# Quads two bodies earlier, an index decode by masks in PSUM, and other places for VectorE's low halves in a trunk's PEER layers

## The chip, the cores and the metric

The kernel runs on one core of a Trainium2 chip. The metric is the device time of one execution in microseconds (us). Each count given as "x" is a number of instructions. Five engines work beside each other and wait for each other by semaphores: TensorE (PE), VectorE (DVE), ScalarE (ACT), GpSimd (POOL) and SyncE (SP), which issues the DMA transfers.

## The reference

A decoder trunk of two layers on x of 256 tokens by 1024 channels, all float32. A layer adds two things to x. The first is a mixer (retention, RWKV-7 and gated linear attention behind one projection). The second is PEER, a retrieval over 128 x 128 = 16,384 experts of one neuron each:

```python
q = (xb @ w_q).reshape(p, 8, 2, 128)
sc = jnp.einsum('thpc,hpnc->thpn', q, sub_keys)
s1, i1 = lax.top_k(sc[:, :, 0], 16)
s2, i2 = lax.top_k(sc[:, :, 1], 16)
cand = s1[..., :, None] + s2[..., None, :]
cand_idx = i1[..., :, None] * 128 + i2[..., None, :]
top_s, sel = lax.top_k(cand.reshape(p, 8, 256), 16)
gate = softmax(top_s)
act = gelu(einsum('td,ted->te', xb, u[eidx])) * gate
out = einsum('te,ted->td', act, v[eidx])
```

So each token has 8 heads with 16 chosen experts each. A token's expert is found by a row index i1 and a column index i2.

## The kernel before

**The dense form.** The kernel doesn't gather. It computes the activations of all 16,384 experts for all 256 tokens (u half), multiplies them with a dense matrix of gates that is zero where a token didn't choose an expert, and multiplies the result with all of v (v half). In each layer the u half comes in 32 **bodies** of four expert groups of 128, each body in eight **halves** m = 0 to 7 (four of the eight channel chunks each). Float32 weights are split in two parts of lower precision: ACT casts a half's weights from the ring w_ring into expert_hi (u_split, L976), DVE or POOL subtracts to make expert_lo (the **low**, L1656 on DVE, L1826 on POOL), and PE makes 12 products of 128x128 by 256 columns (u_half, L783 to L785). There are four buffers for the parts, so the cast of a half waits until PE has done the half four before it. The v half has the same form (v_split L1047, v_lows L1660, a_split L1056, a_lows L1664, v_half L814 to L816). SP reloads the two ring slots of 1 MB when the lows of their last halves are made.

**Who makes the lows.** In bodies 1 to FREE - 1 = 10, DVE makes the lows of halves 2 and 6 (D_FEW) by few_lows, at places written by hand into the sort, and POOL makes the other six (P_MANY). From body FREE = 11 on DVE makes six (D_MANY) and POOL two (P_FEW).

**The sort (topk, L1567).** While PE works on bodies 0 to 10, DVE takes the scores SC (32 rows of 128 per token tile set), and for two halves t of them finds the 16 largest of each row: 16 max operations, 16 pairs of max_index and match_replace, 16 max again, 16 max_index again. Then stage1_done is signalled, the 50 candidates per head are built (CAND, L1595 to L1605), and the 16 best with their places POS are found in the same way. The gates' differences are signalled (gdiff_ready). ACT takes the exponential at a fixed place of its own order, behind body EXP_BODY - 1 = 8 (L1217); DVE normalises in gates() (L1647), and PE turns the indices and gates (turn_sel) within body FREE.

**The decode.** POS counts through rows of unequal length (16, 8, 5, 4, ... candidates). To find row and column, DVE compares POS with all 16 row starts at once (ISROW, 2048 elements per tile), multiplies with row lengths, index steps and column indices, and reduces each product (L1634 to L1645), for two tiles of 8 heads.

**The quads.** From body QB = 12 on a body also holds three **quads**, each of which makes the gates of four tokens: DVE compares with an iota to get one-hot matrices (hots, L1670), ACT scales them by the gates in eight operations (gate_rows, L1009), PE multiplies (quad, L793 and L794, 8 products), and DVE multiplies the result into the activations (gated, L1678). There are 64 quads and 20 x 3 = 60 of them fit in the bodies; four stand behind the last body. Activations of the bodies before QB (LATE = 48 rows) go straight into ACTS; in later bodies gelu goes back to PSUM (L987) and u_muls (L1685) multiplies it with what the quads so far left in ACTS. For that, unwritten rows of ACTS hold ones: ACT writes them three rows in each body (ones, L1001), eight rows three times later, and POOL writes the rest (L1908). a_split of the first two v groups waits for the last quad and the last u_muls.

**The inverse (invert, L539).** Earlier in the layer the RWKV part inverts 12 triangular matrices of 128 by doubling blocks, level by level. For each level and each of two chunks k, PE makes Y = MASKED x TI (L550), DVE masks it (L1458), PE makes six pairs of small products with TT and Y (L562, L563), and DVE adds them to the halves of TI and TT (L1471). Behind the last level stand transposes (turn_out, L678) and the chunks, which read TT.

The constants of the plan are these:

```python
N_BODY, EXP_BODY, FREE, QB = 32, 9, 11, 12
N_QUAD = S // 4
N_LOOPED = 3 * (N_BODY - QB)
LATE = 4 * QB
```

## Time and profile before

| | us |
|---|---|
| median of 3 runs | 2248.65 |
| lowest and highest run | 2247.8, 2250.03 |
| the profiled execution, its own time | 2248.29 |
| its span, first to last instruction | 2246.5 |
| PE busy | 2128.1 (95%) |
| DVE busy | 1473.0 (66%) |
| ACT busy | 1312.9 (58%) |
| POOL busy | 438.2 (20%) |

The span is that of the profiled execution, from its first to its last instruction; the time is what the device took for the same execution. An engine is busy when one of its instructions runs; a busy time is a union, so overlapping instructions count once. TensorE's granted clock (PEclk) is a share of 2.4 GHz. "Idle before" in a group or a timeline row is how long the engine stood idle before those instructions, with the operation that ended the wait behind the arrow. In layer 0 the u half runs from 337.6 to 755.1 us and the v half from 765.6 to about 1117; layer 1 has the same at 1453.8 and 1883.9. Body 0 starts at 337.6 us, body 1 at 349.1, body 5 at 395.2, body 10 at 469.5 in layer 0.

### The profile page before, as it was taken

What the parts mean: (1) busy time and instruction counts of PE and PEld (TensorE: products, weight loads), DVE (VectorE), ACT (ScalarE), POOL (GpSimd) and SP (SyncE); (2) the same over time, 40 slices, a digit from 0 to 9 for tenths busy, and PEclk for the clock granted to TensorE, in tenths of its full rate; (3) what the DMA queues carried; (4) which work ended last, traced back from release to release, by engine and by line L of the source; (5) the groups of instructions that cost most, each with busy time, mean ns of one, the idle gap of its engine ahead of it and who ended that gap; (6) DMA issues with size and microseconds to landing.
All of it is one profiled execution on the core that took longest, in us unless ns stands there. A gap on an engine that the chain in (4) does not pass through costs nothing.

```text
span 2246.5 us, 45241 instructions
## 1 busy us (share of the span) xinstructions
PE 2128.1 (95%) x14596; PEld 1927.4 (86%) x14596; DVE 1473.0 (66%) x2926; ACT 1312.9 (58%) x3097; POOL 438.2 (20%) x358
## 2 busy tenths in 40 slices
PE   7899899899999899999898998997999998999997
PEld 7889599899999788888787885997999997888886
DVE  5764247968878666666567533489687886666665
ACT  5530145479999755555564302553899996555554
POOL 0312007752222100000004020176522220000000
PEclk9999799999999999999999997998999999999999
DMA  5310244344444355555542102453444443555555
GB/s 222 113 57 1 94 150 171 144 153 168 157 161 168 131 187 194 198 187 192 182 183 94 57 1 94 169 176 124 169 165 155 166 158 141 189 195 194 188 196 186
DMA packets 47459, 338.77 MB, mean 151 GB/s; under 512 B 5648, under 2 KB 5776, under 8 KB 6928
## 3 DMA queue, kind: packets, MB, share of 16 engines
q1 hardware_dynamic: 47376, 337.73, 41.5%
q8 instruction: 44, 0.72, 0.1%
q14 instruction: 39, 0.32, 0.0%
HBM read 336.66 MB, written 1.05 MB: 150 GB/s over the span
## 4 chain that ended last, share of the span: by engine, by line
PE 81%; DVE 8%; issue 4%; POOL 3%; ACT 2%; DMA 2%; DVEq 0%; SPq 0%; POOLq 0%; PEldq 0%; ACTq 0%
PE ps L814 10%; PE ps L815 10%; PE ps L816 10%; PE ps L783 9%; PE ps L785 8%; PE ps L784 8%; POOL expert_lo L1826 3%; PE ps L686 3%; PE ps L407 2%; PE ps L409 2%; PE ps L408 2%; PE ps L550 2%; PE ps L563 1%; PE ps L562 1%; PE ps L793 1%
## 5 line engine op out<-in xcount | busy, mean ns | idle before, releaser
L783 PE MATMUL ps<-h_t_hi,expert_hi 128*128 128x256 f32 x2048 | 595.7, 291 | 27.3 <-DVE expert_lo L1656 22.1
L784 PE MATMUL ps<-h_t_lo,expert_hi 128*128 128x256 f32 x2048 | 582.8, 285 | 0.0
L785 PE MATMUL ps<-h_t_hi,expert_lo 128*128 128x256 f32 x2048 | 582.4, 284 | 0.0
L1826 POOL TENSOR_TENSOR expert_lo<-w_ring,expert_hi 128x512 fp32r<-128x512 f32 x220 | 338.1, 1544 | 763.9 <-ACT expert_hi L976 760.4
L783 PEld LDWEIGHTS ps<-h_t_hi,expert_hi 128*128 128x128 f32 x2048 | 396.0, 193 | 31.9 <-issue 13.3
L814 PE MATMUL ps<-expert_hi,act_hi 128*128 128x512 f32 x1024 | 400.5, 391 | 4.8 <-DVE act_lo L1664 4.8
L815 PE MATMUL ps<-expert_lo,act_hi 128*128 128x512 f32 x1024 | 400.1, 391 | 0.0
L816 PE MATMUL ps<-expert_hi,act_lo 128*128 128x512 f32 x1024 | 400.0, 391 | 0.0
L784 PEld LDWEIGHTS ps<-h_t_lo,expert_hi 128*128 128x128 f32 x2048 | 396.3, 194 | 0.0
L785 PEld LDWEIGHTS ps<-h_t_hi,expert_lo 128*128 128x128 f32 x2048 | 395.9, 193 | 0.0
L976 ACT CAST expert_hi<-w_ring 128x512 fp32r<-128x512 f32 x512 | 308.9, 615 | 141.9 <-PE ps L785 129.1
L1660 DVE TENSOR_TENSOR expert_lo<-w_ring,expert_hi 128x512 fp32r<-128x512 f32 x512 | 331.1, 688 | 0.4
L1056 ACT CAST act_hi<-big 128x256 fp32r (+1 forms) x256 | 103.8, 406 | 329.2 <-PE ps L816 329.2
L1047 ACT CAST expert_hi<-w_ring 128x512 fp32r<-128x512 f32 x512 | 291.3, 617 | 0.0
L1656 DVE TENSOR_TENSOR expert_lo<-w_ring,expert_hi 128x512 fp32r<-128x512 f32 x292 | 213.2, 742 | 116.8 <-ACT expert_hi L976 113.4
L1664 DVE TENSOR_TENSOR act_lo<-big,act_hi 128x256 fp32r<-128x256 f32 x256 | 108.6, 425 | 261.6 <-ACT act_hi L1056 261.6
L814 PEld LDWEIGHTS ps<-expert_hi,act_hi 128*128 128x128 f32 x1024 | 193.3, 189 | 45.5 <-DVE expert_lo L1660 5.3
L815 PEld LDWEIGHTS ps<-expert_lo,act_hi 128*128 128x128 f32 x1024 | 193.3, 189 | 40.1
L816 PEld LDWEIGHTS ps<-expert_hi,act_lo 128*128 128x128 f32 x1024 | 193.1, 189 | 40.1
L938 ACT CAST expert_hi<-w_ring 128x512 fp32r<-128x512 f32 x168 | 99.8, 621 | 119.4 <-PE ps L425 54.5
L1316 DVE TENSOR_TENSOR expert_lo<-w_ring,expert_hi 128x512 fp32r<-128x512 f32 x168 | 119.3, 749 | 67.1 <-ACT expert_hi L938 64.8
L407 PE MATMUL ps<-h_t_hi,expert_hi 128*128 128x256 f32 x448 | 128.3, 286 | 2.4 <-DVE expert_lo L1316 1.0
(293 smaller groups left out, 3359.5 us busy)
## 6 DMA issues: line engine op xcount, KB each, us to landing
w_ring<-u_t SPq DMA_DIRECT2D x128, 1024.0 KB, 4.8
w_ring<-v_t SPq DMA_DIRECT2D x128, 1024.0 KB, 4.8
w_ring<-w_in SPq DMA_DIRECT2D x32, 1024.0 KB, 4.9
w_ring<-w_q SPq DMA_DIRECT2D x16, 1024.0 KB, 4.9
w_ring<-w_out SPq DMA_DIRECT2D x8, 1024.0 KB, 4.8
big<-xconst SPq DMA_DIRECT2D x2, 1666.0 KB, 9.3
w_ring<-keys SPq DMA_DIRECT2D x2, 1024.0 KB, 4.8
big<-rows SPq DMA_DIRECT2D x2, 576.0 KB, 11.3
```

The lines of the kernel that those rows point to most:

```text
L407: pe.matmul(o, w_hi_m[:, c, :], HTH[:, d, :], start=d == 0, stop=False)
L783: pe.matmul(o, w_hi[:, c, :], HTH[:, d, :], start=d == 0, stop=False)
L784: pe.matmul(o, w_hi[:, c, :], HTL[:, d, :], start=False, stop=False)
L785: mm = pe.matmul(o, w_lo[:, c, :], HTH[:, d, :], start=False, stop=d == DC - 1)
L814: pe.matmul(o, a_hi_t, EH[:, m % 4, :], start=start, stop=False, skip_group_check=True)
L815: pe.matmul(o, a_hi_t, EL[:, m % 4, :], start=False, stop=False, skip_group_check=True)
L816: mm = pe.matmul(o, a_lo_t, EH[:, m % 4, :], start=False, stop=True, skip_group_check=True)
L976: act.copy(EH[:, m % 4, :], RING[:, m // 4, (m % 4) * 512:(m % 4 + 1) * 512]).then_inc(u_hi, 1)
L1047: act.copy(EH[:, m % 4, :], RING[:, m // 4, (m % 4) * 512:(m % 4 + 1) * 512]).then_inc(v_hi, 1)
L1656: dve.tensor_tensor(EL[:, m % 4, :], RING[:, m // 4, (m % 4) * 512:(m % 4 + 1) * 512], EH[:, m % 4, :].bitcast(F32), ALU.subtract).then_in ...
L1660: dve.tensor_tensor(EL[:, m % 4, :], RING[:, m // 4, (m % 4) * 512:(m % 4 + 1) * 512], EH[:, m % 4, :].bitcast(F32), ALU.subtract).then_in ...
L1826: pool.tensor_tensor(EL[:, m % 4, :], RING[:, m // 4, (m % 4) * 512:(m % 4 + 1) * 512], EH[:, m % 4, :].bitcast(F32), ALU.subtract).then_i ...
```

## The change

The plan starts the quads at body 10 and ends them within body 31, so the constants move, and bodies 30 and 31 get forms of their own:

```diff
-N_BODY, EXP_BODY, FREE, QB = 32, 9, 11, 12
+N_BODY, EXP_BODY, FREE, QB = 32, 7, 9, 10
 N_QUAD = S // 4
-N_LOOPED = 3 * (N_BODY - QB)
+ONES = 5
@@ PE
-                with pe.Fori(QB, N_BODY) as j:
-                    u_and_quads(j)
-                for q in range(N_LOOPED, N_QUAD):
-                    quad(q % 3, q)
+                with pe.Fori(QB, N_BODY - 1) as j:
+                    u_and_quads(j, (1, 4, 6))
+                u_and_quads(N_BODY - 1, (1,))
@@ ACT
-                with act.Fori(QB, N_BODY - 1) as j:
-                    u_and_gates(j, False)
-                u_and_gates(N_BODY - 1, True)
-                for q in range(N_LOOPED + 2, N_QUAD):
-                    gate_rows(q % 3, q, 0, 8)
+                with act.Fori(QB, N_BODY - 2) as j:
+                    u_and_gates(j, 3, False)
+                u_and_gates(N_BODY - 2, 2, False)
+                u_and_gates(N_BODY - 1, 0, True)
@@ DVE
-                with dve.Fori(QB, N_BODY - 1) as j:
-                    u_and_gated(j, False)
-                u_and_gated(N_BODY - 1, True)
-                for q in range(N_LOOPED, N_QUAD):
-                    gated(q % 3, q, 128 - LATE)
-                    if q + 3 < N_QUAD:
-                        hots(q % 3, q + 3, False)
+                with dve.Fori(QB, N_BODY - 2) as j:
+                    u_and_gated(j, 3, 3, False)
+                u_and_gated(N_BODY - 2, 3, 1, False)
+                u_and_gated(N_BODY - 1, 1, 0, True)
```

ACT writes ones five rows a body instead of three. In the sort DVE's lows stand at other places: one for t = 0 (behind the second maxima) instead of three, four for t = 1 (in the middle of the first maxima, in the middle of the index and replace operations, behind them, and four operations into the second max_index) instead of five, then one behind the candidates, one in the middle of their index and replace operations, one behind their second maxima, one behind their second indices, and four in the decode instead of six. DVE makes 16 of them in all instead of 20.

The decode goes by overwriting. DECODE is a view of PSUM banks 0 to 3 as eight matrices of 256. One mask says where POS has reached row i, and one predicated copy then overwrites the picked value with that of row i:

```diff
+        DECODE = PS[:, 0:4, :].rearrange("p b n -> p (b n)").rearrange("p (m u n) -> p m u n", m=8, u=16)
@@ topk
+                def overwrite(dst, i, src):
+
+                    counted(dve.copy_predicated(dst[:, :, :], DECODE[:, i % 7, :, :].bitcast(U32), src.broadcast_to([P, 16, 16])))
+
+                for i in range(1, 17):
+                    if i < 16:
+                        counted(dve.tensor_scalar(DECODE[:, i % 7, :, :], at, float(ROW_AT[i]), None, ALU.is_ge))
+                    if i > 1:
+                        all_but(1 if i < 16 else 0)
+                        overwrite(PICK, i - 1, ROWKEY[:, :, i - 1:i])
+                    if i == 9:
+                        few_lows(1)
+                all_but(0)
+                few_lows(1)
...
+                for i in range(1, 17):
+                    if i < 16:
+                        counted(dve.tensor_scalar(DECODE[:, i % 7, :, :], at, 128.0 * (i - 1), None, ALU.is_gt))
+                    if i > 1:
+                        all_but(1 if i < 16 else 0)
+                        overwrite(I2F, i - 1, x[:, :, 1, i - 1:i])
+                    if i in (6, 14):
+                        few_lows(1)
+                all_but(0)
```

Here counted() raises the semaphore dve_step by one, and all_but(n) waits until all counted operations but the last n are done. Between the two loops stand five small operations of 256 elements that split the key (row start x 128 + i1) again. The ten products and comparisons of 2048 elements and the six reductions of before, on ISROW and PICKED, are gone.

At the inverse's last level (b = 64) the products and additions into TI are left out, since nothing reads TI after it:

```diff
-                            pe.matmul(PS[:, 4 + 2 * k, h * 64:(h + 1) * 64], TT[:, u, :], first, start=True, stop=True)
+                            if b < 64:
+                                pe.matmul(PS[:, 4 + 2 * k, h * 64:(h + 1) * 64], TT[:, u, :], first, start=True, stop=True)
@@ DVE
-                            ins = dve.tensor_tensor(half, half, zz, ALU.add)
+                            elif i == 1:
+                                half = dst[:, u0:u0 + NH, 64:128]
+                                ins = dve.tensor_tensor(half, half, z.rearrange("p (m b) -> p m b", b=64), ALU.add)
```

## Rows read from the trace of the kernel before

**Rows 1.** The page: the span, and busy time by engine.

```profile
span 2246.5 us, 45241 instructions
...
PE 2128.1 (95%) x14596; PEld 1927.4 (86%) x14596; DVE 1473.0 (66%) x2926; ACT 1312.9 (58%) x3097; POOL 438.2 (20%) x358
```

**Rows 2.** Windows: length; busy us (count) of PE, PEld, DVE, ACT, POOL; PEclk; DMA.

```profile
349.10:395.20 46.10, 46.10 (x386) 46.10 (x385) 38.74 (x212) 26.24 (x51) 31.30 (x24) 1.00 0.53 187
395.20:469.50 74.30, 63.50 (x482) 61.75 (x481) 70.05 (x163) 36.56 (x68) 54.64 (x30) 0.93 0.39 140
507.80:742.10 234.30, 234.30 (x2162) 231.98 (x2161) 190.84 (x291) 227.49 (x651) 55.68 (x36) 1.00 0.45 163
755.14:765.64 10.50, 2.90 (x34) 2.15 (x33) 6.69 (x12) 9.48 (x29) 0.00 (x0) 0.76 0.00 0
765.60:779.10 13.50, 13.46 (x49) 10.93 (x50) 6.58 (x12) 4.35 (x9) 0.00 (x0) 0.81 0.34 116
1511.40:1587.80 76.40, 64.02 (x483) 62.53 (x482) 72.03 (x163) 36.44 (x68) 54.61 (x30) 0.91 0.37 136
```

**Rows 3.** Groups: PE in 391.6 to 472, POOL in 349.1 to 395.2, then 395.2 to 469.5.

```profile
L783 PE MATMUL ps<-h_t_hi,expert_hi 128*128 128x256 f32 x177 | 52.8, 298 | 10.8 <-DVE expert_lo L1656 8.7 <-POOL expert_lo L1826 1.7 <-ACT big L981 0.4
...
L1826 POOL TENSOR_TENSOR expert_lo<-w_ring,expert_hi 128x512 fp32r<-128x512 f32 x24 | 31.3, 1306 | 14.6 <-ACT expert_hi L976 13.4
...
L1826 POOL TENSOR_TENSOR expert_lo<-w_ring,expert_hi 128x512 fp32r<-128x512 f32 x30 | 54.6, 1837 | 18.4 <-ACT expert_hi L976 17.6
```

**Rows 4.** Groups: DVE's lows in 337 to 389.6.

```profile
L1656 DVE TENSOR_TENSOR expert_lo<-w_ring,expert_hi 128x512 fp32r<-128x512 f32 x8 | 5.5, 692 | 12.8 <-ACT expert_hi L976 12.8
```

**Rows 5.** Timeline of DVE: start, us, operation [idle before <-what ended it].

```profile
348.56 0.69 DVE L1656 TENSOR_TENSOR expert_lo<-w_ring,expert_hi 128x512 fp32r<-128x512 f32 x1 [5.55 <-ACT expert_hi L976]
...
395.33 0.69 DVE L1656 TENSOR_TENSOR expert_lo<-w_ring,expert_hi 128x512 fp32r<-128x512 f32 x1
...
403.73 1.41 DVE L1656 TENSOR_TENSOR expert_lo<-w_ring,expert_hi 128x512 fp32r<-128x512 f32 x1
405.06 1.87 DVE L1616 MAX8 h_t<-big 128x8 f32<-128x50 f32 x16
...
411.47 1.16 DVE L1625 CAST h_t<-h_t 128x256 f32<-128x256 uint32 x1
412.66 3.27 DVE L1634 TENSOR_TENSOR big<-h_t,row_consts 128x2048 f32<-128x2048 f32 x1
...
419.27 1.63 DVE L1656 TENSOR_TENSOR expert_lo<-w_ring,expert_hi 128x512 fp32r<-128x512 f32 x1
...
460.80 2.29 DVE L1645 TENSOR_REDUCE h_t<-big 128x128 f32<-128x2048 f32 x1
```

**Rows 6.** Groups by form, DVE, whole span.

```profile
L1553 DVE COPY_PREDICATED big<-big,ps 128x512 f32<-128x512 uint32 x28 | 18.9, 729 | 21.0 <-PE ps L657 20.6 <-DVE big L1530 0.5
...
L1481 DVE COPY big<-ps 128x384 f32<-128x384 f32 x4 | 2.2, 558 | 11.0 <-PE ps L588 11.0
...
L1555 DVE COPY big<-ps 128x256 f32<-128x256 f32 x4 | 1.5, 417 | 0.0
...
L1328 DVE COPY big<-big 128x256 f32<-128x256 f32 x2 | 0.6, 294 | 0.1
```

**Rows 7.** Timeline of the end of the first half of PEER, layer 0.

```profile
755.34 0.37 ACT L987 ACTIVATE ps<-ps 128x256 f32<-128x256 f32 x1 [1.25 <-PE ps L785]
...
762.04 2.17 ACT L1047 CAST expert_hi<-w_ring 128x512 fp32r<-128x512 f32 x4
...
764.10 0.71 ACT L1056 CAST act_hi<-big 128x256 fp32r<-128x256 f32 x2
...
765.64 0.76 PE L814 MATMUL ps<-expert_hi,act_hi 128*128 128x512 f32 x1 [2.41 <-DVE act_lo L1664]
```

**Rows 8.** Timeline of PE: the inverse's last level and the transposes behind it.

```profile
203.34 0.33 PE L562 MATMUL ps<-big 128*128 128x64 f32 x2
...
208.65 1.26 PE L678 MATMUL ps<-const_sb,big 128*128 128x128 f32 x10
```

More of the change, by code:

```diff
@@ L215, in trunk @@
         CAND2 = big(16 * NC).rearrange("p (u n) -> p u n", u=16)
-        ISROW, PICKED = (big(2048).rearrange("p (u k n) -> p u k n", u=8, k=16) for _ in range(2))
-        STEP1 = IDX[:, 0:16, :]
+        ROWKEY = big(256).rearrange("p (u n) -> p u n", u=16)
         ht_flat = HT[:, :, :].rearrange("p c n -> p (c n)")
-        TOPV, POS, POSF, GATE, I1F, I2F, ROWAT, COLF = (ht_flat[:, 256 * i:256 * (i + 1)].rearrange("p (u n) -> p u n", u=16) for i in range(8))
+        TOPV, POS, PICK, GATE, I1F, I2F, PICKI, COLN = (ht_flat[:, 256 * i:256 * (i + 1)].rearrange("p (u n) -> p u n", u=16) for i in range(8))
         ACTS = BIG[:, :].rearrange("p (e t) -> p e t", t=S)
@@ L795, in quad, with u_and_quads @@
                 mm.then_inc(quad_done, 1)
-            def u_and_quads(j):
-                q = 3 * (j - QB)
+            def u_and_quads(j, after):
                 for m in range(8):
                     u_half(m, j, False)
-                    if m in (1, 4, 6):
-                        i = (1, 4, 6).index(m)
-                        quad(i, q + i)
+                    if m in after:
+                        i = after.index(m)
+                        quad(i, 3 * (j - QB) + i)
             def v_half(m, j, first):
@@ L1011, in gate_rows, with u_and_gates @@
                     ins.then_inc(hot_gate, 1)
-            def u_and_gates(j, last):
+            def u_and_gates(j, quads, last):
                 q = 3 * (j - QB)
@@ L1023, in u_and_gates @@
                 u_gelu_late(0, j)
-                gate_rows(2, q + 2, 0, 6)
+                if quads:
+                    gate_rows(2, q + 2, 0, 6)
                 split(6)
@@ L1027, in u_and_gates @@
                 split(7)
-                gate_rows(2, q + 2, 6, 8)
-                gate_rows(0, q + 3, 0, 4)
+                if quads:
+                    gate_rows(2, q + 2, 6, 8)
+                    gate_rows(0, q + 3, 0, 4)
                 split(8)
@@ L1032, in u_and_gates @@
                 u_gelu_late(2, j)
-                gate_rows(0, q + 3, 4, 8)
-                gate_rows(1, q + 4, 0, 2)
+                if quads:
+                    gate_rows(0, q + 3, 4, 8)
+                if quads == 3:
+                    gate_rows(1, q + 4, 0, 2)
                 split(10)
@@ L1037, in u_and_gates @@
                 split(11)
-                gate_rows(1, q + 4, 2, 8)
+                if quads == 3:
+                    gate_rows(1, q + 4, 2, 8)
             def v_split(m, j, first):
@@ L1214, in _ @@
                     u_body(j)
-                    ones(bass.ds(LATE - 3 + 3 * j, 3), 3)
+                    ones(bass.ds(LATE - ONES + ONES * j, ONES), ONES)
                 act.wait_ge(gdiff_ready, 1)
@@ L1580, in topk @@
                         ins = dve.match_replace(SC2[:, u % 16, :], VAL[:, u, 0:8], SC[:, u, :], NEG)
-                        if u % 16 == (7 if t else 11):
+                        if t and u % 16 == 7:
                             few_lows(1)
@@ L1685, in u_muls, with u_and_gated, quad_step, hot_step @@
                 dve.tensor_tensor(a, a, PS[:, 6 + e % 2, 0:S], ALU.mult).then_inc(u_mul, 1)
-            def u_and_gated(j, last):
+            def u_and_gated(j, quads, next_quads, last):
                 q, done = 3 * (j - QB), 4 * (j - QB)
+                def quad_step(i):
+                    if i < quads:
+                        gated(i, q + i, done + i)
+                def hot_step(i):
+                    if i < next_quads:
+                        hots(i, q + 3 + i, False)
+                def next_lows(m):
+                    if not last:
+                        u_lows(m, j + 1)
                 u_lows(4, j)
                 u_lows(5, j)
-                gated(0, q, done)
-                hots(0, q + 3, False)
+                quad_step(0)
+                hot_step(0)
                 u_lows(6, j)
-                u_muls(0, j, q + 1)
-                gated(1, q + 1, done + 1)
-                if not last:
-                    u_lows(0, j + 1)
-                hots(1, q + 4, False)
-                u_muls(1, j, q + 2)
-                if not last:
-                    u_lows(1, j + 1)
-                gated(2, q + 2, done + 2)
-                if not last:
-                    u_lows(2, j + 1)
-                hots(2, q + 5, False)
-                u_muls(2, j, q + 3)
-                u_muls(3, j, q + 3)
+                u_muls(0, j, q + min(1, quads))
+                quad_step(1)
+                next_lows(0)
+                hot_step(1)
+                u_muls(1, j, q + min(2, quads))
+                next_lows(1)
+                quad_step(2)
+                next_lows(2)
+                hot_step(2)
+                u_muls(2, j, q + quads)
+                u_muls(3, j, q + quads)
             norm_rows(0, HN)
```

59 lines of the change are left out of this document (29 added, 30 removed).

## The prediction

> **What bounds the kernel now.** I read the page first. TensorE (PE) is busy for 95% of the span [rows 1]; the reader is to see that only idle or slowed PE time can be won. The windows come second [rows 2]. A body without quads costs PE 46.10/4 = 11.52 us (1.44 us for each of its eight halves), a body with three quads 13.02 us (234.30 us for 18 of them), so a quad costs 1.50/3 = 0.50 us. Two stretches fall short. Bodies 5 to 9 take 74.30 us where five times 11.52 is 57.6: 16.7 us lost in layer 0, and in layer 1 76.40 - 57.6 = 18.8 us. Between the last product of the first half of PEER and the first of the second half lie 10.50 us, with the last four quads in them (the same in layer 1; one of the two rows stands). Third, the group rows for bodies 5 to 9 [rows 3]: PE's waits were ended mostly by DVE's low halves (L1656), and POOL's lows took 1.84 us each, against 1.31 us in bodies 1 to 4. While it sorts and decodes, DVE makes halves 2 and 6 of each body, and it is behind. The kernel is DVE-bound there and PE-bound nearly everywhere else.
>
> My sum goes against the profiled execution: 2248.3 us, of which 2246.5 is the span [rows 1]; it lies 0.4 us under the median of the runs shown, 2248.65.
>
> **Part 1, the inverse.** At the last level (b = 64) PE drops 12 of its 24 small products and DVE two of four additions. The 24 pairs run back to back from 203.34 to 208.65, when the next transposes start [rows 8]: 5.31 us. Half of that is **2.6 us per layer**, if DVE's masked rows, which feed the second half of the products, are ready as early as that; I estimate that they are, since PE doesn't wait there now. The ends are 1.3 us (one of two phases only) and 2.7 us.
>
> **Part 2, the end of the quads.** Bodies 10 and 11 get three quads each, body 31 keeps one, and the four behind the loop go: the same 64 quads, so PE's work is equal, but 4 x 0.50 = 2.0 us of it move out of the gap. What is left in the gap is a chain on ACT and DVE [rows 7]: the last gelu starts 0.2 us after PE's last product, whose end is the window's start (755.34 - 755.14), and ACT goes on 0.3 later (its 0.37 less an overlap); four casts of v take 764.10 - 762.04 = 2.06; the cast of the activations and its low half lead 1.54 us later to the first product (765.64 - 764.10), of which about 0.5 is DVE working off its last gated block, so 1.05. Sum 0.2 + 0.3 + 2.06 + 1.05 = 3.6 us. Gain 10.5 - 3.6 - 2.0 = **4.9 us per layer**. PE's granted clock fell from 2.4 towards 1.2 GHz in that gap (0.76 in the mean over it, 0.81 over the first v body's 13.5 us [rows 2]: 0.19 x 13.5 = 2.6 us of full clock lost there). A gap of 3.6 us may let it fall too; I count no change, with ends of 2 us won and 1 us lost per layer. ACT and DVE carry in bodies 10 and 11 what they carry in 12 to 29 now, and PE was full there: nothing. What the first body with quads costs over the others moves from body 12 to body 10: nothing.
>
> **Part 3, the lows in the sort.** DVE waited 12.8 us for casts before its low halves [rows 4], 5.55 of them before the first, at 348.56 [rows 5]. A low for half m of body j is wanted by PE at 349.1 + 11.52(j-1) + 1.44m, and its cast is there some 3.5 us earlier; one comes due every 5.76 us. With the first low behind the second maxima, DVE gets there at 348.2, and later waits come to about 0.3 us. Up to the low behind the candidates, now at 395.33, fall away 12.8 us of waits and three lows at 0.61; 0.4 + 0.3 of waits and 0.3 for a wider table are added: 395.33 - 12.8 - 1.8 + 1.0 = 381.7. But that low is now the sixth (body 3, half 6), wanted at 380.8.
>
> **Part 4, the decode.** It runs from 411.47 to 463.1 now, 51.6 us with six lows; the big operations of 2048 elements take 2.3 to 3.3 us [rows 5]. In its place come 15 masks and 15 overwrites, twice, of 256 elements. A copy of 256 from PSUM takes 0.417 [rows 6]. An overwrite of 512 takes 0.729; the step from 256 to 384 costs 0.141, so 256 fewer give 0.45. Neighbours overlap by 0.08 (a low ends at 405.14, the next operation starts at 405.06 [rows 5]), so a pair is 0.42 + 0.45 - 0.16 = 0.71, with the waits 0.72. Ends: 0.55, with a mask at the SBUF copy's 0.294 and an overwrite of 0.42; 0.95, if each wait drains DVE (no overlap, 0.04 for each). Sum: 30 x 0.72 = 21.6, steps between 3.0, four lows of 1.2 (between the 0.69 of a free one and the 1.41 and 1.63 of late ones [rows 5]) = 4.8: 29.4 instead of 51.6.
>
> First what the rows show of port and place: a copy of 256 takes 0.294 from SBUF and 0.417 from PSUM [rows 6]. The trace agrees with the Trainium skill (VectorE: DVE Perf Modes, "Why PSUM operands drop a tier"), which speaks against this change: a PSUM operand costs fp32 copies their double rate. By it masks in SBUF would be 0.12 us cheaper each, 3.7 us per layer. Against that stand POOL's lows, 1.31 us beside the sort and 1.84 beside the decode [rows 3]. The Trainium skill (SBUF — State Buffer, "🔬 SBUF: two separate sides") gives a lock that GpSimd shares with DVE operations of two SBUF inputs or a two-port mode; by it masks and overwrites with a PSUM side neither wait for POOL nor hold it up.
>
> **The stalls that stay.** Between the lows DVE has 1.9 us for 16 maxima, 5.9 for 16 index and replace operations (395.33 to 403.73 less a low and the maxima), 3.0 for the second indices (406.93 to 411.47 less a low and the difference of 0.5) [rows 5]. A late low costs 1.2, and every stall moves what PE wants next. Low by low (DVE's start, its end, PE's want, the stall):
> sixth 381.7, 382.8, 380.8: 2.0; seventh (1.9 + 2.9 on) 387.6, 388.8, 388.5: 0.3; eighth (2.9 + 1.9 on) 393.6, 394.8, 394.6: 0.2; ninth 397.8, in time, then 0.7 + 0.5 + 0.9 to the decode's start at 399.9; tenth (0.35 and 8 pairs) 406.0, 407.2, 406.3: 0.9; eleventh (7 pairs) 412.3, 413.5, 413.0: 0.5; twelfth (2.1, 0.35 and 5 pairs) 419.5, 420.7, 419.2: 1.5; thirteenth (8 pairs) 426.5, 427.7, 426.5: 1.2. Two more pairs and 1.5 for the gates end at 430.7, the fourteenth is wanted at 433.4, and the decode is over before body 9. **6.6 us per layer stay** of 16.7 and 18.8. Bounds: 2.5 (lows at 0.69, pair 0.60) and 12.6 (pair 0.95: 30 x 0.23 = 6.9 later, of which some 6 reach PE). Gain 10.1 + 12.2 = **22.3 us**. ACT now waits for the differences of the gates behind body 6, whose end is at 349.1 + 6 x 11.52 = 418.2 at the earliest; DVE has them at about 399: nothing, and should it come after 418, casts and so PE stop. ACT's five slices of ones instead of three per body fall into its idle time (26.2 of 46.1 us busy [rows 2]): nothing.
>
> **Sum.** 2248.3 - 5.2 - 9.8 - 22.3 = **2211.0 us**.
>
> **Rivals.**
> A, the forecast above: 0.66.
> B, nearly no stall stays (2.5 us per layer) and the clock holds in the gap: 2211.0 - 8.2 - 4 = 2199. For it: the 12.8 us of DVE's waits are simply gone [rows 4]; against: the sixth low is late by the order alone. 0.15.
> C, the decode is dearer: masks and overwrites drain each other at 1.1 us a pair, 30 x 0.38 = 11.4 us later per layer, stalls of about 18 as now. Only parts 1 and 2 are left: 2233. For it: every overwrite waits on a counter; against: a chained operation starts 0.03 us behind the one it waits for (412.63, 412.66 [rows 5]). 0.11.
> D, the gap doesn't shrink, since something else (v's transfer, the order of ACT's casts) holds the first product: 2221. 0.04.
> E, slower: overwrites stand behind POOL's lows. A DVE low grew from 0.69 to 1.63 beside busy POOL, by 0.94 us [rows 5]. If all 30 pairs paid it, the decode ends 28 us later and 6.6 + 28 = 34.8 us are lost per layer: 2248.3 - 15.0 + 69.6 - 35.5 = 2267. It decides from 1.34 us a pair (0.62 over mine), where the extra 18.6 us per layer use up all gains. Against: POOL is busy for only 54.64 of 74.30 us there [rows 2], and not every operation can meet it. 0.04.
>
> **Numbers.** About 0.2% (4.5 us) is what a measurement can tell from no change. The range takes in A with its bounds (2199 to 2225) and B; C and E are left out, with D inside. Faster 0.95, same 0.01, slower 0.04.
>
> **What would show it.** Bodies 5 to 8 (with body 3) should lose 6 to 7 us over 11.52 each, with PE's waits there still ended by the DVE low of halves 6; the gap between the halves of PEER should be 3.6 us with no quad in it; the overwrites should start 0.7 us apart; POOL's lows should be back at 1.3 us; the transposes behind the inverse should start at about 206.0. Wrong would be a pair over 1 us, a decode that ends behind 441 (the start of body 9), or a gap over 6 us.

## The result and the profile after

The changed kernel takes **2197.5 us** in the median of four runs (2193.7 to 2201.7), against 2248.7 before: ratio 0.977 (0.975 to 0.980), 51 us less where 37.3 were forecast. The time lies just under the range. One execution of inv_dve, further down, took 2951.1 us at a mean granted clock of 0.658 and is left out of its ratio. The profiled execution took 2193.71 us, 54.6 less than the one that the prediction summed against. The page of after:

```profile
PE 2094.9 (96%) x14548; PEld 1900.6 (87%) x14548; DVE 1442.1 (66%) x3050; ACT 1314.0 (60%) x3093; POOL 388.7 (18%) x342
PE 86%; DVE 9%; ACT 2%; DMA 2%; issue 1%; SPq 0%; DVEq 0%; ACTq 0%; PEldq 0%
L784 PE MATMUL ps<-h_t_hi,expert_hi 128*128 128x256 f32 x2048 | 591.3, 289 | 12.4 <-DVE expert_lo L1685 8.6
L1865 POOL TENSOR_TENSOR expert_lo<-w_ring,expert_hi 128x512 fp32r<-128x512 f32 x204 | 289.7, 1428 | 772.6 <-ACT expert_hi L975 770.9
```

To see where the 54.6 us went, I cut both executions at the first product of each half of PEER (u: first half, v: second):

| stretch | before | after | less | forecast |
|---|---|---|---|---|
| start to first u product, layer 0 | 337.6 | 328.8 | 8.8 | 2.6 |
| first u to first v product, layer 0 | 428.0 | 411.9 | 16.1 | 15.0 |
| last v body to first u product, layer 1 | 348.3 | 337.8 | 10.5 | 2.6 |
| first u to first v product, layer 1 | 430.1 | 411.8 | 18.3 | 17.1 |
| first v body, layer 0 (in layer 1 0.2 more, not less) | 13.4 | 12.6 | 0.8 | 0 |

The two stretches with parts 2 to 4 came out nearly as forecast: 34.4 us against 32.1. Of the 17.3 us beyond the forecast, 14.1 lie ahead of PEER (19.3 us against 5.2), where the change touches only the inverse. Windows of after: first bodies 5 to 9 with their transposes, in each layer (74.30 and 76.40 us before [rows 2]):

```profile
387.30:450.50 63.20, 59.39 (x488) 58.47 (x487) 40.94 (x89) 43.49 (x76) 36.24 (x25) 1.00 0.50 175
1476.10:1539.20 63.10, 59.37 (x489) 58.43 (x487) 40.85 (x89) 43.56 (x76) 36.31 (x25) 1.00 0.48 174
```

and the POOL group over the same stretch, whose mean was 1837 ns before [rows 3]:

```profile
L1865 POOL TENSOR_TENSOR expert_lo<-w_ring,expert_hi 128x512 fp32r<-128x512 f32 x24 | 31.7, 1329 | 27.5 <-ACT expert_hi L975 27.1
```

The gap between the halves, in the timeline of after (compare [rows 7]): no quad is left in it, and it lasts 3.5 us.

```profile
737.04 0.28 PE L786 MATMUL ps<-h_t_hi,expert_lo 128*128 128x256 f32 x1
737.36 0.37 ACT L986 ACTIVATE ps<-ps 128x256 f32<-128x256 f32 x1 [2.51 <-PE ps L786]
737.63 2.17 ACT L1051 CAST expert_hi<-w_ring 128x512 fp32r<-128x512 f32 x4
739.70 0.71 ACT L1060 CAST act_hi<-big 128x256 fp32r<-128x256 f32 x2
740.71 0.47 PE L814 MATMUL ps<-expert_hi,act_hi 128*128 128x512 f32 x1 [3.39 <-DVE act_lo L1693]
```

The decode on DVE (L1651 and L1668 make masks, L1647 overwrites): a pair every 0.68 us, start to start, from 390.07 to 417.9. The first row is the sixth low, ahead of it.

```profile
370.98 1.67 DVE L1685 TENSOR_TENSOR expert_lo<-w_ring,expert_hi 128x512 fp32r<-128x512 f32 x1
...
390.07 0.77 DVE L1651 TENSOR_SCALAR ps<-ps 128x256 f32<-128x256 f32 x2
390.74 0.45 DVE L1647 COPY_PREDICATED h_t<-ps,big 128x256 f32<-128x256 uint32 x1
391.08 0.44 DVE L1651 TENSOR_SCALAR ps<-ps 128x256 f32<-128x256 f32 x1
391.42 0.45 DVE L1647 COPY_PREDICATED h_t<-ps,big 128x256 f32<-128x256 uint32 x1
...
395.83 1.44 DVE L1685 TENSOR_TENSOR expert_lo<-w_ring,expert_hi 128x512 fp32r<-128x512 f32 x1
...
417.00 0.94 DVE L1647 COPY_PREDICATED h_t<-ps,big 128x256 f32<-128x256 uint32 x2
```

Not every stall that is left is DVE's. Bodies 3, 5 and 6 wait for its low halves; body 7 waits for ACT, whose exponential (L1221) stands behind body 6 now and has a table load of 1.28 us before and behind it. The waits of PE that end in these bodies, with ACT's two loads:

```profile
372.78 0.38 PE L784 MATMUL ps<-h_t_hi,expert_hi 128*128 128x256 f32 x1 [0.56 <-DVE expert_lo L1685]
397.40 0.38 PE L784 MATMUL ps<-h_t_hi,expert_hi 128*128 128x256 f32 x1 [1.25 <-DVE expert_lo L1685]
410.89 0.38 PE L784 MATMUL ps<-h_t_hi,expert_hi 128*128 128x256 f32 x1 [1.70 <-DVE expert_lo L1685]
416.14 1.28 ACT L1221 ACT_TABLE_LOAD   x1
418.90 1.28 ACT L980 ACT_TABLE_LOAD   x1
420.63 0.38 PE L784 MATMUL ps<-h_t_hi,expert_hi 128*128 128x256 f32 x1 [0.69 <-ACT big L980]
```

Now the inverse and the chunk part behind it. PE's timeline in after: the last level's small products take 2.63 us (205.11 to 207.74) instead of 5.31 [rows 8].

```profile
205.11 2.79 PE L564 MATMUL ps<-big 128*128 128x64 f32 x24
207.74 1.26 PE L679 MATMUL ps<-const_sb,big 128*128 128x128 f32 x10
209.96 1.55 PE L581 MATMUL ps<-big 128*128 128x64 f32 x12 [0.96 <-ACT h_t L1188]
```

The windows of the chunk part, from these transposes (L679) to the output projection's twelve matmuls that follow it. Columns: stretch, length, busy us of PE, PEld, DVE, ACT, POOL, PEclk, DMA. First before, then after:

```profile
208.65:241.35 32.70, 31.74 (x168) 24.87 (x167) 4.26 (x11) 1.41 (x4) 0.00 (x0) 0.74 0.00 1
```

```profile
207.74:233.08 25.34, 24.38 (x169) 19.14 (x168) 3.79 (x10) 1.41 (x4) 0.00 (x0) 0.99 0.00 1
```

The same products take 7.4 us less, since PE's granted clock was at 1.2 GHz for 20.5 us over this part before (224.6 to 245.1), and for 3.4 us at its end after (from 232.8). Such a stretch at 1.2 GHz is called a spell below, and those that begin over the chunk part are the long ones (17 to 24 us) or the short ones (3 to 7 us).

### The profile page after: what moved, and what is told of

It is laid out like the page before. It is cut to its first block, busy times and chain, and to the rows that moved or that the text cites. A ratio compares the mean times of both kernels' runs of the same rounds, so it can differ in the third digit from the quotient of the medians.

```text
span 2191.9 us, 45295 instructions
## 1 busy us (share of the span) xinstructions
PE 2094.9 (96%) x14548; PEld 1900.6 (87%) x14548; DVE 1442.1 (66%) x3050; ACT 1314.0 (60%) x3093; POOL 388.7 (18%) x342
## 4 chain that ended last, share of the span: by engine, by line
PE 86%; DVE 9%; ACT 2%; DMA 2%; issue 1%; SPq 0%; DVEq 0%; ACTq 0%; PEldq 0%
PE ps L814 11%; PE ps L815 11%; PE ps L816 11%; PE ps L784 10%; PE ps L786 9%; PE ps L785 9%; PE ps L687 2%; PE ps L407 2%; PE ps L408 2%; PE ps L409 2%; PE ps L550 2%; PE ps L564 1%; PE ps L794 1%; PE ps L423 1%; PE ps L795 1%; DVE expert_lo L1319 1%
## 5 line engine op out<-in xcount | busy, mean ns | idle before, releaser
L1865 POOL TENSOR_TENSOR expert_lo<-w_ring,expert_hi 128x512 fp32r<-128x512 f32 x204 | 289.7, 1428 | 772.6 <-ACT expert_hi L975 770.9
L784 PEld LDWEIGHTS ps<-h_t_hi,expert_hi 128*128 128x128 f32 x2048 | 391.6, 191 | 15.7 <-ACT big L980 8.4
L786 PEld LDWEIGHTS ps<-h_t_hi,expert_lo 128*128 128x128 f32 x2048 | 391.6, 191 | 0.0
```

The source lines that it names most:

```text
L784: pe.matmul(o, w_hi[:, c, :], HTH[:, d, :], start=d == 0, stop=False)
L786: mm = pe.matmul(o, w_lo[:, c, :], HTH[:, d, :], start=False, stop=d == DC - 1)
L1865: pool.tensor_tensor(EL[:, m % 4, :], RING[:, m // 4, (m % 4) * 512:(m % 4 + 1) * 512], EH[:, m % 4, :].bitcast(F32), ALU.subtract).then_i ...
```

## The experiments

**Splitting the change.** Edits: inv_only is the kernel before with only the inverse's edit; no_inv the kernel after with that edit taken back; inv_dve the kernel before with only DVE's two additions dropped.

```diff
 # inv_only, PE's part; no_inv is the reverse, on the kernel after
-                            pe.matmul(PS[:, 4 + 2 * k, h * 64:(h + 1) * 64], TT[:, u, :], first, start=True, stop=True)
+                            if b < 64:
+                                pe.matmul(PS[:, 4 + 2 * k, h * 64:(h + 1) * 64], TT[:, u, :], first, start=True, stop=True)
...
```

> The kernel before, with the inverse's part of the change alone. Theory C (clock): leaving out 12 products per layer saves 2 x 2.65 us of PE time and also shortens the stretch at half clock behind the inverse (20.5 us in each layer before, 3.4 after), so the time falls by 12 to 20 us, to 2229 to 2237, and at least one of the two long stretches is gone in the profile. Theory D (direct only): the clock stretches have nothing to do with these products; the time falls by 5.3 us to 2243.4 and both stretches stay at about 20 us.

> The changed kernel, with the inverse's part undone. Theory C: it loses what inv_only wins, 12 to 20 us against the median of the changed kernel (2197.5): 2210 to 2218, with long stretches at half clock in both layers. Theory D: 5.3 us are lost, 2203, and the stretches stay short in part of the executions.

> The kernel before, with DVE's two needless additions of the inverse's last level left out and PE's products kept. Both theories: the next PE work waits for the products and not for these additions, so the time stays within 1 us of 2248.7 and both clock stretches stay at 20 us. A fall of 5 us or more would put the gain on DVE's side.

Measured: inv_only 2233.2 us (2227.0 to 2244.1), ratio 0.994 (0.992 to 0.997); no_inv 2214.5 (2213.0 to 2215.3), 0.986 (0.984 to 0.988); inv_dve 2248.9, 1.001 (0.999 to 1.003). So PE's twelve products per layer carry most of the surprise: leaving them out is worth 14.7 us on before (2247.9 beside these runs) and 17.0 on after, three times the 5.3 us that they take, and the 9.4 and 11.7 us beyond that stand against a surprise of 13.9 in the medians (51.2 less 37.3). DVE's additions are worth nothing. In inv_only's trace layer 1 has a half-clock spell of 3.4 us over the chunk part and layer 0 one of 17.1; no_inv has 20.5 us in both layers:

```profile
208.70:241.50 32.80, 31.84 (x169) 24.93 (x168) 4.26 (x11) 1.41 (x4) 0.00 (x0) 0.74 0.00 0
```

One output product in no_inv at 1.2 GHz (two matmuls in the trace) took 2.02 us:

```profile
229.86 2.02 PE L686 MATMUL ps<-w_ring,h_t 128*128 128x512 f32 x2
```

and the same product in after, at 2.4 GHz, 1.08:

```profile
226.46 1.08 PE L687 MATMUL ps<-w_ring,h_t 128*128 128x512 f32 x2
```

The kernel before isn't bound to the long spell either. It was measured again beside each group of runs, with medians of 2245.9 to 2248.7 us, but 9 of these 61 executions took only 2233.4 to 2239.5, which inv_only takes too. They have no trace; that they lack a long spell is my guess from their higher mean clock (0.969 to 0.974 where the others mostly have 0.965 to 0.967).

**Part 2 alone**: late_quads is after with the quads where they were before, four of them behind the loop, and with them the exponential (behind body 8), three rows of ones a body and four more lows ahead of the gates.

```diff
-N_BODY, EXP_BODY, FREE, QB = 32, 7, 9, 10
+N_BODY, EXP_BODY, FREE, QB = 32, 9, 11, 12
...
```

> The changed kernel with the plan's constants as before (quads from body 12 on, FREE 11, EXP_BODY 9, four quads behind the last body), the new decode, the new places of the lows and the short inverse kept, with four more lows ahead of the gates. My sum for part 2 says that it loses 2 x 4.9 = 9.8 us against the changed kernel, 2207, with gaps of 10.5 us between the halves of PEER. A loss under 4 us would say that the quads' place is worth little; over 14 us, that the earlier end of the quads also kept the clock up.

Measured: 2202.0 us (2199.6 to 2208.2), ratio 0.980 (0.978 to 0.982). First u to first v product takes 416.1 us in both layers against 411.9 in after, and the gap is 10.5 again: part 2 is worth 4.2 us per layer in the trace, where 4.9 were forecast. The gap alone gives 10.5 - 3.5 - 2.0 = 5.0; the other 0.8 are lost in bodies 3 to 9, where late_quads stalls for 4.7 us and after for 5.5. It also shows whose the stall in body 7 is: with the exponential behind body 8, body 7 loses 0.2 us instead of 1.1, and body 9 loses 0.7. The time alone (4.5 us over after, with overlapping ranges) can't say this, since this profile has a long spell over the chunk part in layer 0 (23.9 us) and a short one in layer 1.

**Width or place of the work.** wide12 puts twelve unread products of 256 columns where the narrow ones were dropped; shift12 puts them ahead of the first inverse level; shift_mid ahead of the units, some 16 us earlier.

```diff
 # shift12, behind pe.wait_ge(mrow_out, 4) in invert()
+                for i in range(12):
+                    pe.matmul(PS[:, 1 + 2 * (i // 6), 256:512], ident, XC[:, 0:256], start=True, stop=True)
```

> The kernel after, with each of the twelve narrow products (64 columns) that the last inverse level dropped replaced by one of 256 columns into a part of PSUM that nobody reads. The phase takes again the 5.3 us of before (or up to 1 us more), so the direct part of the gain, 2.65 us per layer, is undone. What it tells apart is why the half-clock spell over the chunk part shrank. Theory (density): TensorE was thinly used, and long narrow stretches bring the spell; wide products keep it short, 3.4 us in both layers, and the kernel takes about 2195 + 5 to 7 = 2201 us. Rival 1 (length or place): the spell depends on when the work comes, not on how wide it is; then it is 17 us or more again as in no_inv, and the time is near that one's 2214.5. Rival 2: dummy products hold up the copies out of PSUM, and the time goes over 2216.

> The kernel after, with the last inverse level still short, and twelve products of 256 columns (about 2.7 us) put ahead of the first inverse level, so that everything from there on starts 2.7 us later. Theory (the stretch itself decides): the spell over the chunk part stays at 3.4 us, and the kernel takes 2197.5 + 5.4 = 2203 us. Rival (place in time decides): with the chunk part back at the time of before the spell is 17 us or more again, and it takes about 2214. If PE's extra products lie beside a wait that it had anyway, the cost is less, 2198.

> The kernel after, with twelve products of 256 columns (about 2.7 us) put ahead of the units, some 16 us before the inverse, instead of right ahead of the inverse as in shift12. Theory (place in time): the chunk part starts up to 2.7 us later and the half-clock spell over it is again 17 us or more; 2210 to 2215 us, as shift12. Rival (what lies between the idle time at 157 to 160 us and the chunk part decides, not the time itself): the spell stays at 3.4 us; 2203 us. If DVE's copies hide the products, nothing moves, 2198, and the run tells nothing.

My size was off in all three: such a product takes 0.45 us where nothing stands between, so twelve take 5.4 us and not 2.7. Measured: wide12 2212.0 us (ratio 0.985, 0.983 to 0.986), spells of 3.4 + 3.4 and 6.8 + 6.8 us; shift12 2214.7 (0.986, 0.984 to 0.987), 20.5 us in both layers, although its last level is as short as in after; shift_mid 2208.4 (2200.0 to 2213.1; 0.984, 0.981 to 0.987), 6.8 us in both. So the twelve narrow products aren't needed for the long spell; work far ahead of the chunk part brings it too. Wide work in its place gives something in between. shift_mid's time also holds a stall of 5.2 us in body 3 of both layers: the eight additions that make DVE's candidates took 5.61 us beside five POOL lows in a row (2.32 in after), and the low behind them came late.

```profile
371.53 7.36 POOL L1867 TENSOR_TENSOR expert_lo<-w_ring,expert_hi 128x512 fp32r<-128x512 f32 x5 [1.47 <-ACT expert_hi L977]
371.83 5.61 DVE L1607 TENSOR_TENSOR big<-big 128x256 f32<-128x256 f32 x8
```

**PSUM or SBUF for the masks**: masks_sbuf.

```diff
-        DECODE = PS[:, 0:4, :].rearrange("p b n -> p (b n)").rearrange("p (m u n) -> p m u n", m=8, u=16)
+        DECODE = big(2048).rearrange("p (m u n) -> p m u n", m=8, u=16)
```

> The kernel after, with the masks, the positions and the column numbers of the decode in SBUF (beside the row keys) instead of the four PSUM banks. Theory 1 (the PSUM operand costs more than the port lock saves): masks take about 0.30 us instead of 0.43, the decode is 3 to 4 us shorter, POOL's lows stay near 1.3 to 1.4 us, and 2 to 3 us per layer of the stalls in bodies 7 and 8 go: 2192 to 2195 us. Theory 2 (the lock that GpSimd shares with DVE costs more): operations of DVE grow beside POOL's lows, to 0.5 us and more, POOL's lows grow to over 1.6 us, and the time is 2205 us or more. In between, 2196 to 2200, neither outweighs the other.

Measured: 2211.0 us (2200.3 to 2213.0), ratio 0.982 (0.980 to 0.984). First u to first v product takes 416.0 and 418.3 us, 4.1 and 6.5 more than in after. DVE's timeline shows both theories at once: free of POOL the mask takes 0.28 us, but up to 1.39 beside a POOL low, and the overwrite 0.43 or 1.55.

```profile
390.71 1.55 DVE L1647 COPY_PREDICATED h_t<-big 128x256 f32<-128x256 uint32 x1
392.16 1.39 DVE L1651 TENSOR_SCALAR big<-big 128x256 f32<-128x256 f32 x1
393.47 0.44 DVE L1647 COPY_PREDICATED h_t<-big 128x256 f32<-128x256 uint32 x1
393.81 0.28 DVE L1651 TENSOR_SCALAR big<-big 128x256 f32<-128x256 f32 x1
...
400.28 0.68 DVE L1685 TENSOR_TENSOR expert_lo<-w_ring,expert_hi 128x512 fp32r<-128x512 f32 x1
```

By the Trainium skill (SBUF — State Buffer, "🔬 SBUF: two separate sides") GpSimd shares a lock with DVE's operations in a two-port mode or with two SBUF inputs. By the Trainium skill (VectorE: DVE Perf Modes, "Why PSUM operands drop a tier") a PSUM operand keeps a float32 operation from the faster rate. The trace agrees with both, and here the lock weighs more: with masks in SBUF their mean is 0.55 us and the overwrites' 0.62. In after, with masks in PSUM, 36 of the 60 masks and 40 of the 60 overwrites ran beside a POOL low too, and still the means are 0.43 and 0.45 us and no operation took over 0.47.

**The stalls that stay**: lows_tuned moves six low halves ahead, lows_tuned2 chooses all places again from its trace.

```diff
 # lows_tuned2, first decode loop; the other places go in the same way
-                    if i == 9:
+                    if i in (7, 14):
                         few_lows(1)
```

> The kernel after, with six of DVE's low halves moved ahead by some 2 to 4 us each: the sixth into the making of the candidates, the tenth and eleventh behind masks 7 and 14 of the first decode loop, the twelfth ahead of the second loop, the thirteenth and fourteenth behind masks 8 and 16 of it. Theory (those lows are late by their place in the order): the stalls of bodies 3 and 5 to 8, 5.5 us per layer now, fall to 1 to 2 us, and the kernel takes 2197.5 - 8 = 2190 us. Rival (DVE has too much work there, and moving lows ahead only moves the lateness to the next): stalls stay at 4 us or more, 2195 or more.

> As lows_tuned, with the places chosen again from its trace, where the seventh low had come 3 us late: sixth in the making of the candidates, seventh in the middle of the maxima, eighth behind the eleventh index, ninth ahead of the second indices, tenth ahead of the decode, then behind masks 7 and 14 of the first loop, masks 2 and 9 of the second, and the fifteenth behind it. Theory: of the 4.4 us per layer that still stall in lows_tuned under 1 us is left in bodies 3 to 8; against after 5 us less per layer in the sort and decode, 2188 us if the front is as in after. Rival (too little slack: earlier lows now wait for their casts and delay those behind): 2 us or more stay stalled per layer.

Measured: lows_tuned 2192.4 us (2186.7 to 2202.8), ratio 0.976 (0.973 to 0.978); the sixth low is on time, but now the seventh comes late, at 377.86, and body 4 loses 3.2 us: 4.4 per layer in all, so that the rival came true. lows_tuned2 2191.7 (2183.9 to 2198.7), 0.976 (0.973 to 0.979); only body 7 still loses 1.1 us, which is ACT's, and first u to first v product takes 407.6, 4.3 us less than in after. The profile is its slowest run, 2198.7, with spells of 23.9 us in both layers. Less twice 7.4 that is 2183.9, its fastest run, and two of the other four lie halfway (2191.4 and 2191.9): no, one or two layers with the long spell, as I read it. The last two, 2187.9 and 2196.0, lie between these levels.

**Unread products in idle time**: fillers puts them behind the output projection, between the halves of PEER and at the end of a layer; best1 is fillers with the lows of lows_tuned2; best2 is best1 with fitting counts.

```diff
 # best2; fillers and best1 had 7, 13 and 28
                 project_out()
+                for i in range(4):
+                    pe.matmul(PS[:, 0, :], ident, XC[:, 0:512], start=True, stop=True)
...
+                for i in range(7):
+                    pe.matmul(PS[:, 3, 0:256], ident, KONST[:, 0:256], start=True, stop=True)
...
                 pe.sem_inc(arrived, 1)
+                for i in range(16):
+                    pe.matmul(PS[:, 4, 0:256], ident, KONST[:, 0:256], start=True, stop=True)
```

> The kernel after, with products that nobody reads in three idle stretches of TensorE: 7 of 512 columns behind the output projection (idle 4.1 us now), 13 of 256 columns between the halves of PEER (3.5 us), 28 of 256 columns at the end of a layer (7.7 us). Theory (the clock falls because TensorE is idle): the spells at 263.5 (10.2 us), 741.4 (3.4), 1093.0 (13.7) and their like in layer 1 go; behind the idle times 8.5, 3.4 and 8.4 us run at half clock now, which costs half of that, 4.2 + 1.7 + 4.2 in layer 0 and 4.2 + 1.7 in layer 1 = 16 us at most; less about 1 us where a product ends late: 2183 us. Rival (products on zeros or on an idle bank don't hold it, or they delay the work behind): 2197 or more.

> The kernel after with the low places of lows_tuned2 and the idle-time products of fillers. If both are worth what they are alone and don't meet, 2197.5 - 10 - 15 = 2173 us; if the products shift the chunk part of layer 1 into a long spell, 2180.

> As best1, with the idle-time products cut to fit: the trace of fillers showed 0.89 us for one of 512 columns and 0.45 for one of 256, twice what I had reckoned. Now 4, 7 and 16 of them, 3.6, 3.1 and 7.2 us in idle times of 4.1, 3.5 and 7.7. Gain over after: lows 5.0 us per layer; the first v body 1.5 us per layer; the stage behind the second norm 3.3 per layer; the second layer's start 4.2: 10 + 3 + 6.6 + 4.2 = 23.8, so 2173.7 us, give or take 7.5 for the spell over the chunk part.

Measured: fillers 2199.2 us, ratio 0.981 (0.979 to 0.984); best1 2198.0, 0.979 (0.975 to 0.982); **best2 2183.0 (2174.9 to 2183.7), 0.971 (0.968 to 0.973)**, faster than after by 14.5 us, with ranges that don't touch. All three missed their forecasts (2183, 2173 and 2173.7 give or take 7.5). In fillers the spells behind the three idle times are gone, but the products were twice too long and held up what follows (6.25 us where 4.1 was idle). With fitting counts (best2) the spells behind them are gone, but for 3.4 us at the end of layer 0, and the next work starts on time. Windows of the wait for the second norm, the stage behind it, the gap, and the first v body; after, then best2:

```profile
261.20:265.20 4.00, 0.00 (x0) 0.00 (x0) 2.40 (x6) 3.13 (x6) 0.00 (x0) 0.79 0.70 233
265.20:275.40 10.20, 8.77 (x32) 7.53 (x33) 5.98 (x12) 6.93 (x14) 0.00 (x0) 0.58 0.33 117
737.20:740.70 3.50, 0.12 (x2) 0.02 (x1) 2.28 (x5) 3.06 (x7) 0.00 (x0) 1.00 0.26 108
740.70:751.70 11.00, 10.99 (x41) 8.91 (x42) 5.09 (x10) 3.70 (x8) 0.00 (x0) 0.84 0.33 104
```

```profile
260.80:264.70 3.90, 3.67 (x8) 1.43 (x8) 2.31 (x6) 3.03 (x6) 0.00 (x0) 1.00 0.67 235
264.70:274.90 10.20, 8.35 (x46) 7.37 (x47) 7.28 (x14) 7.03 (x14) 0.00 (x0) 1.00 0.33 119
729.30:732.90 3.60, 3.24 (x16) 2.54 (x16) 2.28 (x5) 3.06 (x7) 0.00 (x0) 1.00 0.28 118
732.90:743.90 11.00, 11.00 (x48) 9.09 (x49) 6.54 (x12) 4.35 (x9) 0.00 (x0) 1.00 0.39 141
```

**Why the long spell comes or not.** Up to here the time of unbroken work from PE's last wait to the chunk part mostly went with it. drop32 drops twelve more small products (those of the first half at b = 32, so that the additions read old values and the inverse is left wrong in part; only its time counts), fill_units fills the wait ahead of the inverse, best3 is best2 with the same filling, rest_long and rest_best put a wait in the middle of the inverse, into no_inv and best2.

```diff
 # drop32
-                            if b < 64:
+                            if b < 32:
 # fill_units, behind the transposes of BT and KT
+                for i in range(4):
+                    pe.matmul(PS[:, 6, 0:256], ident, KONST[:, 0:256], start=True, stop=True)
 # rest_long, rest_best, on DVE behind its wait for z_done
+                        if n == 3 and k == 0:
+                            for i in range(9):
+                                link(dve.tensor_tensor(EL[:, 0, 0:256], KONST[:, 0:256], KONST[:, 0:256], ALU.subtract))
```

> The kernel after without another twelve of PE's small products, those of the first half at level b = 32 (the additions then read old values, so the inverse is left wrong in part). From the first product of the inverse to the chunk part it is then some 45.2 us instead of 47.8, and 50.7 before the change. Theory (the length of uninterrupted thin work since the idle time ahead of the inverse decides; at 50.7 us the long spell came in all layers, at 47.8 in about half): at 45.2 it comes in none. Then both layers have the short spell, and the runs lie close together at 2194 - 5.3 = 2188.5 us. Rival (it is an even draw for each layer whenever the twelve products are gone): half-clock spells of over 20 us go on in about half of the layers, and the runs spread from 2188 to 2203 us.

> The kernel after with four products that nobody reads, of 256 columns each and 1.8 us together, in the 2.0 us in which TensorE waits ahead of the inverse. They move the last idle time ahead of the chunk part 3 us earlier and delay nothing. Theory (length since the last idle time decides): the chunk part then begins over 50.7 us behind the last idle time, as before the change, and the long spell is back in both layers; the short spell at 157.7 gets no longer: about 2209 us. Rival (denser work holds the clock up): the spell at 157.7 shrinks or goes, the chunk part stays as in after, 2193 us or less.

> best2 with the four products of fill_units as well. If dense work holds the clock up there, 2 to 3 us per layer under best2; if they bring the long spell over the chunk part back in both layers, 7 us over best2's median.

> The kernel no_inv (after with the twelve products left in; 2214.5 us, the long spell in both layers) with nine subtractions of 256 elements that nobody reads on DVE, ahead of the additions of inverse level b = 16, so that TensorE stands idle for about 2 us in the middle of the inverse. Theory (the length of work since the last idle time decides): the last idle time is now some 25 us ahead of the chunk part instead of 50, and the spell over it is short (under 7 us) in both layers, which gives back 7.5 us per layer; the wait costs 2.2 and the half-clock spell it brings by itself 1.7 to 3.4 per layer: about 2214.5 + 2 x (4 to 5.5) - 15 = 2208 to 2210 us. The sign is in the spells rather than in the time. Rival (the long spell comes from the amount of thin work, and rest does not matter): the spell stays at 17 us or more, and the time is 2222 us or more.

> The kernel best2 with the same wait in the middle of the inverse. Theory: short spells in both layers in every run, so runs close together at 2174.9 (best2's lowest, taken as the one with two short spells) + 2 x 4 to 5.5 = 2183 to 2186 us. Rival: long spells go on in about half of the layers, 2190 us or more in the median with a spread of 8 to 15.

Measured: drop32 2192.8 us (2189.2 to 2196.9), ratio 0.976 (0.974 to 0.978); fill_units 2203.5, 0.980 (0.979 to 0.982); best3 2184.5, 0.971 (0.969 to 0.973); rest_long 2215.8, 0.987 (0.984 to 0.989); rest_best 2204.8, 0.981 (0.978 to 0.984). drop32 has no long spell, but its runs lie no closer together than before. PE's wait in the last two was 5.4 us, not 2, and brought a spell of 10.2 us of its own (from 195 us), which ends 10 to 13 us ahead of the transposes; so their spells are the part to read, not their times. The profiles' layers, sorted by the time from the end of PE's last wait to the transposes:

| kernels | from the last wait, us | spell over the chunk part, us |
|---|---|---|
| before, inv_dve, no_inv, shift12 | 50.6 to 53.7 | 20.5 in all 8 layers |
| wide12 | 53.0 to 53.1 | 3.4 + 3.4; 6.8 + 6.8 |
| fill_units | 49.7 | 6.8 + 6.8; 20.5 |
| best3 | 49.4 | 20.5 in both |
| after, the seven others with its inverse, inv_only | 46.9 to 48.1 | 3.4 in 10 layers, 17 to 24 in 8 |
| shift_mid, drop32 | 45.3 to 47.2 | 3.4 to 6.8 in all 4 |
| rest_long | 18.8 | 6.8 in both |
| rest_best | 16.1 to 16.3 | 20.5 in both |

Most rows speak for the length. Two speak against it: wide12 has the longest stretch but for one layer and no long spell, and in rest_best the long spell came in both layers 16 us behind a wait.

```profile
215.90:248.00 32.10, 31.14 (x168) 24.39 (x167) 3.80 (x10) 1.41 (x4) 0.00 (x0) 0.76 0.00 1
```

rest_long, with nearly the same wait, had the short one in both, in place of the 20.5 us of no_inv:

```profile
218.30:244.20 25.90, 24.94 (x168) 19.67 (x167) 4.27 (x11) 1.41 (x4) 0.00 (x0) 0.97 0.00 1
```

So the theory of the length falls as a rule. What all traces share is this: the clock falls either 15 to 17 us behind the start of the transposes and stays down for 17 to 24 us, or 24 to 26 us behind it, for 3 to 7 us (wide12 and a layer of fill_units had two short ones, from 16 to 17 and from 26 to 27 us). It isn't a property of the text alone, since one kernel shows both in its two layers (late_quads, masks_sbuf, best2). Taking 2.65 us out of what lies ahead, or putting 2 to 5 us in, changed how often it came; what decides between the two in a given layer stays open. fill_units also shows the rival's side: the spell ahead of the inverse shrank from 6.8 to 3.4 us, and best3, with no such spell left in its profile, is no faster than best2 because of its two long ones.

## Why the prediction was wrong, and where it was right

- **The step that failed is part 1**, "2.6 us per layer". The direct term was right: 5.31 us of small products became 2.63, and the ends 1.3 and 2.7 held it. But I gave the end of the stretch to the transposes and didn't ask at which clock the work behind them ran. That work lay at 1.2 GHz for 20.5 us, and taking twelve products away ahead of it won another 7.4 us in each layer in which the spell became short: 19.3 us ahead of PEER in the profiled execution instead of 5.2, and 14.7 and 17.0 us in the medians of inv_only and no_inv. The term should have had ends of 2.6 and some 10 us per layer. The fast side of the range, 2199, was drawn without it. The prediction says itself that idle or slowed PE time can be won, but looked for slowed time only in PEER and its gap. Its slow side, by its own ends, adds up to 2227.6 and not 2225, which changes nothing here.
- **Part 2** was right in mechanism and nearly in size: a gap of 3.5 us against 3.6, which makes 5.0 us per layer against 4.9, and 4.2 in all by late_quads.
- **Parts 3 and 4** were right in the main, and in part by luck: stalls of 5.5 us per layer in bodies 3 to 8, against 6.6. Body by body: 0.8, 0.1, 1.5, 2.0, 1.1 and 0 measured, 2.0, 0.5, 0.9, 2.0, 1.2 and 0 forecast. The 1.1 of body 7 is not the late thirteenth low of my sum: ACT's table loads, exponential and five rows of ones (1.26 us, where three took 0.83) hold it up, which I had put at nothing, and it stays at 1.1 in lows_tuned2, where all lows are on time. A pair took 0.68 us against 0.72. The sixth low started 2 us earlier in relation to PE than in my sum, since the additions that make the candidates took 2.32 us instead of 4.68, but took 1.67 us instead of 1.2.
- **The decode's place**: it ran from 390.07 to 417.9, 28 us instead of 51.6, against 29.4 forecast; POOL's lows fell to 1.33 us as the signs said. Rivals C and E (pairs of 1.1 and 1.34 us) are out. masks_sbuf shows what E was afraid of, once the PSUM side is taken away.
- **Rival B** named nearly this time (2199), but for another reason: its stalls (2.5 us) and its clock in the gap didn't come; 5.5 us stayed, and the clock still fell at 741.4.
- The transposes behind the inverse started at 207.7 and not at 206.0, since the last level began 1.8 us later than before (205.11 against 203.34); this lateness was there ahead of the inverse, whose first product came at 160.0 instead of 157.8. Relative to the level's start the 2.6 us are there.

## What to carry to other kernels

Before pricing work that is taken from a thin stretch, look at the granted clock of the stretch behind it: a half-clock spell there made the term three times as large here, and uncertain, so give it its own end in the range. An idle wait of 3 to 8 us on PE was paid twice here, as idle time and as half clock behind it; unread products cut to the length of the wait held the clock, and those that stood over its end held up what follows. Masks that DVE makes and reads beside busy GpSimd work were cheaper in PSUM, although making one alone is dearer there (0.43 us against 0.28).

## What the runs showed that I had not expected

- The length of a half-clock spell in one and the same stretch differed between layers and executions of one kernel (3.4 or 23.9 us), and with it the time from the transposes to PEER (121.1 or 128.5 us in late_quads).
- Products on an idle bank held the clock at 2.4 GHz in idle times of 3.5, 4.1 and 7.5 us, and removed half-clock spells of 3.4, 10.2 and 10.3 of 13.7 us.
- At 2.4 GHz a plain float32 product of 256 columns takes 0.45 us and one of 512 takes 0.89: seven of these took 6.25 us and stand as fourteen matmuls in the trace of fillers.
- A predicated copy of 256 elements with its mask in SBUF took 0.43 us alone and 1.55 beside a GpSimd operation, but never over 0.47 in after, where the mask came from PSUM.
- The ones, the exponential and its two table loads (1.28 us each) on ScalarE cost TensorE 1.1 us in the body in which they stand (0.7 us with three rows of ones instead of five), and the loss moved with them to another body.
